# State-space scan turned so that features lie on the output partitions, with the z projections inside the scan and a shorter output stage

## The chip, the core and the metric

The kernel runs on one core of a Trainium2 chip. The metric is the device time of one launch in microseconds. Engines are called by the names of the profile: PE is TensorE's matmuls, PEld its weight loads, DVE is VectorE, ACT is ScalarE, POOL is GpSimd, SP is the queue that issues most transfers.

## The reference, cut to what matters

One encoder layer runs over two sequences of 256 and 512 tokens (768 in all, 6 tiles of 128), model width 1024. The part that the change touches is the state-space branch:

```python
xbc = silu(conv7(xbc) + conv_b)            # 2048 x-features, 512 B, 512 C
xs = xbc[:2048] -> (tokens, 4 groups, 8 heads, 64)
for each direction (forward, backward):
    dt = softplus(dt_raw + dt_bias);  a_cum = cumsum(-exp(a_log) * dt) in chunks of 128
    y_diag[l] = sum_s (C_l . B_s) * exp(a_cum[l] - a_cum[s]) * dt[s] * x[s]     # s on one side of l
    states    = B^T (exp(a_end - a_cum) * dt * x), carried from chunk to chunk
    y_off[l]  = exp(a_cum[l]) * C_l . h_in
y = (y_fwd + y_bwd + d_skip * xs) * silu(z)
s_out = rmsnorm(y, ssm_norm) @ w_out_ssm;  merged = sigmoid(gate_s) * s_out + sigmoid(gate_a) * a_out
```

Query, key and value projections, windowed attention, a second gated output, a mixing product with routing, and a mixture of 32 experts follow. They keep their instructions.

## The kernel before, in words

Every engine runs its own written-out program; semaphores order them. Every stage begins and ends with a barrier. The work comes as **pieces**: 128 output columns of a weight matrix, 128x1024 per partition. SP loads a piece, ACT rounds it to a high part (`round`, L446), an elementwise pass subtracts to get the low part (`lower`, L451, on POOL), and PE multiplies three ways (high by high, low by high, high by low: `products`, L164). A piece takes 48 matmuls, 24 with 256 moving columns and 24 with 512. There are two buffers: piece n+2 is rounded when PE has finished piece n.

`ssd_groups` runs over four groups of heads. A **prologue** projects and convolves the six tiles of group 0. Then each group has a **head** (transposes of x and B, the products of C with B, eight chunk states carried along the chain) and six **steps**, one for each chunk of 128 tokens. In step t:

- PE projects a tile of the next group, multiplies C by the entering states (L648), waits for `decay_ok`, and multiplies the decays by x (16 products, L654).
- POOL subtracts the cumulative sums (`differences`, L737), makes dt*x and skip*x (`inputs`, L746 and L748), and lowers a piece.
- DVE multiplies the decays by C.B (`decay`, L807), caps the differences (`cap`, L802), gathers the chunk's result (`output`, L814 to L820), and convolves the next group's tile (`convolve`, L790 and L794, seven passes over 774 elements).
- ACT moves the projection out of the banks (`leave`, L673), rounds a piece, applies silu (L681), and makes one exponential over 2048 elements (`decay`, L685).

Tokens lie on the partitions of y, which goes to memory. `ssm_branch` then has 40 pieces: 16 z tiles (each with six transposes of y, L1000), the first halves of w_out for eight output tiles between the two halves of z, and eight pairs of gate and second half. `GatedOutput` makes these pairs.

## Time and profile before

| | us |
|---|---|
| median of 3 runs (2384.92 to 2391.55) | 2385.72 |
| the profiled execution's own time | 2384.32 |
| its span | 2382.6 |
| PE busy | 1873.8 (79%) |
| DVE busy | 868.8 (36%) |
| POOL busy | 627.5 (26%) |
| ACT busy | 551.8 (23%) |
| mean granted clock of TensorE | 0.841 of 2.4 GHz |

The busy shares are averages over stages that have different limits; the scan and the output stage are read by themselves below. The profiled execution is 1.4 us under the median.

### The profile page before, as it was taken

What the parts mean: (1) busy time and instruction counts of PE and PEld (TensorE: products, weight loads), DVE (VectorE), ACT (ScalarE), POOL (GpSimd) and SP (SyncE); (2) the same over time, 40 slices, a digit from 0 to 9 for tenths busy, and PEclk for the clock granted to TensorE, in tenths of its full rate; (3) what the DMA queues carried; (4) which work ended last, traced back from release to release, by engine and by line L of the source; (5) the groups of instructions that cost most, each with busy time, mean ns of one, the idle gap of its engine ahead of it and who ended that gap; (6) DMA issues with size and microseconds to landing.
All of it is one profiled execution on the core that took longest, in us unless ns stands there. A gap on an engine that the chain in (4) does not pass through costs nothing. (4 is left out here: it accounts for less than half of the span.)

```text
span 2382.6 us, 24844 instructions
## 1 busy us (share of the span) xinstructions
PE 1873.8 (79%) x8894; PEld 1299.0 (55%) x8894; DVE 868.8 (36%) x1168; ACT 551.8 (23%) x935; POOL 627.5 (26%) x394
## 2 busy tenths in 40 slices
PE   4968688685798999989889888979657786777771
PEld 3746477473687787877667777754312222222220
DVE  2779789696721122217622222211310000000002
ACT  3223223132132132126544433101100000000000
POOL 4267374753843253221100002210020000000002
PEclk7978788887599999999955558999778889988886
DMA  3313322323232231211188002222389999999994
GB/s 108 101 37 83 84 62 57 93 67 84 79 100 66 67 95 53 62 47 42 44 182 172 1 1 71 62 100 71 124 343 404 385 404 398 407 395 413 391 401 164
DMA packets 228718, 376.18 MB, mean 158 GB/s; under 512 B 9072, under 2 KB 185328, under 8 KB 219824
## 3 DMA queue, kind: packets, MB, share of 16 engines
q1 hardware_dynamic: 221504, 351.90, 43.2%
q0 software_dynamic: 6720, 21.50, 2.4%
q10 hardware_dynamic: 432, 1.96, 0.2%
q8 instruction: 37, 0.61, 0.1%
q14 instruction: 25, 0.20, 0.0%
HBM read 324.81 MB, written 48.96 MB: 157 GB/s over the span
## 5 line engine op out<-in xcount | busy, mean ns | idle before, releaser
L1898 PE MATMUL bank<-e_w,e_xT 128*64 128x512 f32 x1088 | 288.2, 690 | 125.3 <-DMA e_w<-in_w_up 123.9
L164 PE MATMUL bank<-h_high,w_w_high 128*128 128x256 f32 x960 | 342.3, 357 | 35.4 <-issue 7.7
L164 PE MATMUL bank<-h_low,w_w_high 128*128 128x256 f32 x960 | 332.6, 346 | 0.0
L164 PE MATMUL bank<-h_high,w_w_low 128*128 128x256 f32 x960 | 331.3, 345 | 0.0
L451 POOL TENSOR_TENSOR w_w_low<-w_raw,w_w_high 128x1024 fp32r<-128x1024 f32 x76 | 192.1, 2529 | 483.3 <-ACT w_w_high L446 483.3
L1898 PEld LDWEIGHTS bank<-e_w,e_xT 128*64 128x64 f32 x1088 | 92.9, 158 | 299.3 <-issue 232.6
L164 PEld LDWEIGHTS bank<-h_high,w_w_high 128*128 128x128 f32 x960 | 192.5, 200 | 64.5 <-issue 38.8
L794 DVE SCALAR_TENSOR_TENSOR ssd_xc<-ssd_conv_in,ssd_conv_p,ssd_xc 128x774 f32<-128x774 f32 x144 | 205.6, 1428 | 10.8
L164 PEld LDWEIGHTS bank<-h_low,w_w_high 128*128 128x128 f32 x960 | 192.4, 200 | 18.8 <-issue 2.4
L164 PEld LDWEIGHTS bank<-h_high,w_w_low 128*128 128x128 f32 x960 | 191.6, 200 | 19.3
L1956 POOL DMA_DIRECT2D rows_out<-e_y x68 | 36.3, 534 | 554.3 <-ACT e_y L1951 552.3
L654 PE MATMUL bank<-ssd_x_dt,ssd_decays 128*128 128x64 f32 x768 | 125.3, 341 | 48.2 <-DVE ssd_decays L807 41.0
L654 PEld LDWEIGHTS bank<-ssd_x_dt,ssd_decays 128*128 128x128 f32 x768 | 123.2, 255 | 67.6 <-DVE ssd_decays L807 50.5
L737 POOL TENSOR_TENSOR ssd_decays<-ssd_decays,ssd_tables 128x1024 f32<-128x1024 f32 x48 | 114.8, 2413 | 120.3 <-DMA ssd_decays<-decay_sums 120.3
L451 POOL TENSOR_TENSOR att_out_w_low<-att_out_raw,att_out_w_high 128x1024 fp32r<-128x1024 f32 x16 | 39.0, 2442 | 364.7 <-ACT att_out_w_high L446 364.7
L1918 PE MATMUL bank<-e_wd,e_actT 128*64 128x512 f32 x544 | 123.5, 596 | 1.7 <-issue 1.7
L685 ACT ACTIVATE ssd_decays<-ssd_decays 128x2048 f32<-128x2048 f32 x24 | 45.9, 1911 | 315.4 <-DVE ssd_decays L802 315.4
L1946 ACT ACTIVATE e_silu<-bank 128x256 f32<-128x256 f32 x34 | 13.0, 383 | 410.4 <-PE bank L1898 410.4
L446 ACT ACTIVATE w_w_high<-w_raw 128x1024 fp32r<-128x1024 f32 x76 | 80.6, 1061 | 118.6 <-PEq L460 114.7
L1925 DVE COPY e_xT<-bank 128x512 f32<-128x512 f32 x34 | 21.9, 686 | 225.4 <-PE bank L1886 225.4
L1485 PEld LDWEIGHTS bank<-v,att_pT 128*128 128x128 f32 x448 | 103.0, 322 | 0.0
L1932 DVE TENSOR_TENSOR e_act<-e_silu,bank 128x256 f32<-128x256 f32 x34 | 14.2, 416 | 241.6 <-ACT e_silu L1946 241.6
(253 smaller groups left out, 3068.2 us busy)
## 6 DMA issues: line engine op xcount, KB each, us to landing
e_w<-in_w_gate SPq DMA_DIRECT2D x34, 2048.0 KB, 15.1
e_w<-in_w_up SPq DMA_DIRECT2D x34, 2048.0 KB, 19.6
e_wd<-in_w_down SPq DMA_DIRECT2D x34, 2048.0 KB, 10.8
w_raw<-in_w_in SPq DMA_DIRECT2D x60, 512.0 KB, 4.6
ssd_decays<-decay_sums SPq DMA_DIRECT2D x48, 512.0 KB, 5.8
rows_in<-zeros SPq DMA_DIRECT2D x4, 3584.0 KB, 43.6
e_x<-rows_in SPq DMA_DIRECT2D x17, 512.0 KB, 11.1
rows_out<-e_y POOLq DMA_DIRECT2D x68, 128.0 KB, 6.1
```

The source lines that it names most:

```text
L164: last = pe.matmul(out, lhs[k][a], rhs[k][b], start=(k == 0 and m == 0), stop=(k == n - 1 and m == 2))
L446: act.activation(self.pair[u].high[:, :, :], self.raw[u][:, :, :], ACT.Copy).then_inc(self.rounded, 1)
L451: pool.tensor_tensor(self.pair[u].low[:, :, :], self.raw[u][:, :, :], self.pair[u].high[:, :, :].bitcast(F32), ALU.subtract).then_inc(self ...
L654: last = pe.matmul(core.bank[2 + t % 2][:, e * SP_:(e + 1) * SP_], decays[t % NDEC][:, d, e, :], x_dt[t % 2][:, d, e * SP_:(e + 1) * SP_], ...
L685: act.activation(decays[t % NDEC][:, :, :, :], decays[t % NDEC][:, :, :, :], ACT.Exp).then_inc(exp_ok, 1)
L737: last = pool.tensor_tensor(decays[t % NDEC][:, d, :, :], decays[t % NDEC][:, d, :, :], heads(table(g, "cum", t, d), P), ALU.subtract)
L794: last = dve.scalar_tensor_tensor(xc[:, ct, :], x[:, k:k + CONV], conv_p[:, ct, k:k + 1], xc[:, ct, :], ALU.mult, ALU.add)
L1485: last = pe.matmul(core.bank[4 + 2 * (t % 2) + head // 8][:, at:at + HD], pT[m % 4][:, b * P:(b + 1) * P], core.v[:, lo + b, kv * HD:(kv + ...
L1898: last = pe.matmul(core.bank[2 + u][half * CAP:(half + 1) * CAP, :], xT[:, k, u * CAP:(u + 1) * CAP], w[u][:, :, k, half * HALF:(half + 1) ...
L1918: last = pe.matmul(core.bank[6 + u][half * CAP:(half + 1) * CAP, :], act_T[u][:, k % 2, k // 2, :], wd[u][:, k, half * 512:(half + 1) * 51 ...
L1925: last = dve.tensor_copy(xT[:, 4 * j:4 * j + 4, :], core.bank[j][:, :].rearrange("p (k r) -> p k r", k=4))
L1956: pool.dma_start(core.rows_out[bass.ds(n * CAP, CAP), half * 512:(half + 1) * 512], y[u][half * CAP:(half + 1) * CAP, :]).then_inc(y_out[u ...
```

## The change

The scan is turned. x stays with its features on the partitions, and so does y. The diagonal part takes x of a head (128x64) as the weights and the decays (128 columns) as the moving operand; the two heads of a pair write partitions 0 to 63 and 64 to 127 of one bank. The entering states are weights in four blocks of 128x128, and C is the moving operand.

dt is taken into the exponent: a table `start` holds log dt minus the cumulative sum, and one exponential per head and direction takes it as its per-partition bias (16 passes over 128 elements in place of one over 2048). The cap becomes a minimum with the cumulative sum itself, so that POOL's subtraction goes, and so do dt*x; the skip is folded into x by ACT (four passes per group). exp(a_cum) comes from memory, copied over 64 partitions (`reach`).

POOL has nothing left in the scan and the output stage: lowering the pieces, making `x_end` and summing the squares go to DVE. The 16 z pieces move from the stage behind into the scan, by the list `ssd_schedule`; y is multiplied by silu(z) there, and goes to memory transposed. The stage behind, `ssm_output`, loads y in 16 tiles without transposing it, and has 24 pieces, over three pairs of banks. The scan is written out in full instead of in a loop over two of its groups.

At the start of the kernel the constants and the row of parameters are loaded in part; the rest comes in the query stage and the mixing stage. `step_sizes` makes one more logarithm and writes exp(a_cum) to memory.

```diff
+def ssd_schedule():
+
+    prologue = [("c", 0, ct) for ct in range(GC)]
+    prepare = [[] if g == 0 else [("z", g - 1, 2), ("z", g - 1, 3)] for g in range(SG)]
+    steps = []
+    for g in range(SG - 1):
+        c = [("c", g + 1, ct) for ct in range(GC)]
+        z = [("z", g, hp) for hp in range(2)]
+        steps.append([c[0:2], c[2:3], [c[3], z[0]], c[4:5], c[5:6], z[1:2]])
+    steps.append([[("z", SG - 1, hp)] for hp in range(4)] + [[], []])
+    return prologue, prepare, steps
...
+                def project(n, s):
+
+                    if s == 0:
+                        w.ready(pe, n)
+                    if n >= 2:
+                        pe.wait_ge(left, 2 * (n - 2) + s + 1)
+                    last = products(pe, core.bank[2 * (n % 2) + s][:, 0:SEQS[s]], w.parts(n % 2),
+                                    h_parts(core, FIRST[s] * P, SEQS[s]))
+                    last.then_inc(proj_mm if s == 0 else w.used, 1)
+
+                def both(piece):
                     for s in range(2):
-                        pe.wait_ge(left, 2 * (GC * g + ct) + s + 1)
-                        last = products(pe, core.bank[s][:, 0:SEQS[s]], w.parts(ct % 2),
-                                        h_parts(core, FIRST[s] * P, SEQS[s]))
-                        last.then_inc(proj_mm, 1)
...
+                def chunk(g, t):
+                    if t == 0:
+                        pe.wait_ge(cb_ok, 2 * g + 2)
+                        pe.wait_ge(st_ok, NST * g + NST)
+                    else:
+                        pe.wait_ge(y_ok, NT * g + t)
+                    for d in ENTERED[t]:
+                        for q in range(HP):
+                            pe.matmul(core.bank[6 + d][:, q * P:(q + 1) * P],
+                                      state[:, ENTERS[t, d], q * P:(q + 1) * P], xc[g % 2][:, POS[t]:POS[t] + P],
+                                      start=True, stop=True)
+                    pe.wait_ge(decay_ok, NT * g + t + 1)
+                    for q in range(HP):
+                        for d in range(2):
+                            for e in range(2):
+                                h = 2 * q + e
+                                last = pe.matmul(core.bank[4 + t % 2][SP_ * e:SP_ * (e + 1), q * P:(q + 1) * P],
+                                                 xs[:, t, h * SP_:(h + 1) * SP_], decays[t % 2][:, d, h, :],
+                                                 start=(d == 0), stop=(d == 1))
+                    last.then_inc(y_mm, 1)
+
+                for piece in PROLOGUE:
+                    both(piece)
+                for g in range(SG):
+                    if g:
+                        both(PREPARE[g][0])
+                    transposes(g)
+                    states(g, range(0, 3))
+                    if g:
+                        project(NUMBER[PREPARE[g][1]], 0)
+                    states(g, range(3, 6))
+                    if g:
+                        project(NUMBER[PREPARE[g][1]], 1)
+                    states(g, range(6, NST))
                     for t in range(NT):
-                        if more:
-                            project(g + 1, t)
-                        if t >= 2:
-                            pe.wait_ge(y_ok, NT * g + NT + t - 1)
-                        for d in range(2):
-                            if (t, d) in ENTERS:
-                                pe.matmul(core.bank[off_banks(t)[d]][:, :], cT[:, POS[t]:POS[t] + P],
-                                          state[:, ENTERS[t, d], :], start=True, stop=True)
-                        pe.wait_ge(decay_ok, NT * g + t + 1)
-                        pe.wait_ge(xdt_ok, NT * g + t + 1)
-                        for e in range(HPG):
-                            for d in range(2):
-                                last = pe.matmul(core.bank[2 + t % 2][:, e * SP_:(e + 1) * SP_],
-                                                 decays[t % NDEC][:, d, e, :],
-                                                 x_dt[t % 2][:, d, e * SP_:(e + 1) * SP_],
-                                                 start=(d == 0), stop=(d == 1))
-                        last.then_inc(y_mm, 1)
-
-                pe.sem_inc(y_mm, NT)
-                for ct in range(GC):
-                    project(0, ct)
-                groups(pe, scan)
+                        for piece in STEPS[g][t]:
+                            both(piece)
+                        chunk(g, t)
...
                 def decay(g, t):
                     act.wait_ge(capped, NT * g + t + 1)
-                    act.activation(decays[t % NDEC][:, :, :, :], decays[t % NDEC][:, :, :, :], ACT.Exp).then_inc(exp_ok, 1)
...
+                    for d in range(2):
+                        for h in range(HPG):
+                            at = g * HPG + h
+                            e = decays[t % 2][:, d, h, :]
+                            last = act.activation(e, e, ACT.Exp, bias=core.tab["start"][:, t, d, at:at + 1])
+                    last.then_inc(exp_ok, 1)
...
                 def cap(g, t):
 
-                    dve.wait_ge(diff_ok, NT * g + t + 1)
-                    flat = decays[t % NDEC][:, :, :, :].rearrange("p d e l -> p (d e l)")
-                    dve.tensor_scalar(flat, flat, 0.0, None, ALU.min).then_inc(capped, 1)
+                    dve.wait_ge(sums_in[t % 2], 16 * (NT // 2 * g + t // 2 + 1))
+                    to = core.tab["cum"][:, t, :, g * HPG:(g + 1) * HPG].unsqueeze(3).to_broadcast([P, 2, HPG, P])
+                    dve.tensor_tensor(decays[t % 2][:, :, :, :], decays[t % 2][:, :, :, :], to, ALU.min)\
+                        .then_inc(capped, 1)
 
                 def decay(g, t):
                     dve.wait_ge(exp_ok, NT * g + t + 1)
-                    for d in range(2):
-                        last = dve.tensor_tensor(decays[t % NDEC][:, d, :, :], decays[t % NDEC][:, d, :, :],
-                                                 cb[:, d, t, :].unsqueeze(1).to_broadcast([P, HPG, P]), ALU.mult)
-                    last.then_inc(decay_ok, 1)
+                    dve.tensor_tensor(decays[t % 2][:, :, :, :], decays[t % 2][:, :, :, :],
+                                      cb[:, :, t, :].unsqueeze(2).to_broadcast([P, 2, HPG, P]), ALU.mult)\
+                        .then_inc(decay_ok, 1)
 
...
                 def output(g, t):
...
+                    i = NT * g + t
...
+                    out = xx[g % 2][:, :, POS[t]:POS[t] + P]
+                    tiles = "p (q l) -> p q l"
+                    dve.wait_ge(y_mm, i + 1)
...
+                        dve.tensor_tensor(part[:, :].rearrange(tiles, l=P), core.bank[6 + d][:, :].rearrange(tiles, l=P),
+                                          reach[t % 2][:, d, :, :], ALU.mult)
+                        if n == 0:
+                            dve.tensor_tensor(out, out, core.bank[4 + t % 2][:, :].rearrange(tiles, l=P), ALU.add)
+                        dve.drain()
+                        last = dve.tensor_tensor(out, out, part[:, :].rearrange(tiles, l=P), ALU.add)
+                        dve.drain()
                     last.then_inc(y_ok, 1)
...
+                def gate(g, hp):
+                    dve.wait_ge(left, 2 * NUMBER["z", g, hp] + 2)
+                    out = xx[g % 2][:, hp, :]
+                    dve.tensor_tensor(out, out, gate_tile(g, hp), ALU.mult).then_inc(gated, 1)
...
+                    for t in range(NT):
+                        decay(g, t)
+                        pieces = STEPS[g][t]
+                        if pieces:
+                            lower_ahead(pieces[0])
+                        if t:
+                            output(g, t - 1)
+                        elif g:
+                            gate(g - 1, 3)
+                        if t + 1 < NT:
+                            cap(g, t + 1)
+                        if len(pieces) > 1:
+                            lower_ahead(pieces[1])
+                        if g + 1 < SG:
+                            convolve(g + 1, t)
+                    dve.drain()
+                output(SG - 1, NT - 1)
+                for hp in range(HP):
+                    gate(SG - 1, hp)
...
+def output_order():
+
+    order = [("gate", 0), ("gate", 1)] + [("half", c) for c in range(D // P)] + [("gate", 2)]
+    for c in range(D // P):
+        order.append(("branch", c))
+        if c + 3 < D // P:
+            order.append(("gate", c + 3))
+    return order
```

VectorE in step 1 of a group. In the names, `ssd_decays` holds the decays of the chunk, `ssd_y` (before) and `ssd_x` (now) the output, and L790/L794 and L842/L845 are the convolution. Before:

```order
L807 TENSOR_TENSOR ssd_decays<-ssd_decays,ssd_cb 128x1024 [waits ssd_exp_ok]
L807 TENSOR_TENSOR ssd_decays<-ssd_decays,ssd_cb 128x1024
L802 TENSOR_SCALAR ssd_decays<-ssd_decays 128x2048 [waits ssd_diff_ok]
L814 TENSOR_TENSOR ssd_y<-ssd_y,bank 128x512 [waits ssd_y_mm]
L817 TENSOR_TENSOR ssd_part<-bank,ssd_tabs 128x512
L820 TENSOR_TENSOR ssd_y<-ssd_y,ssd_part 128x512
L790 TENSOR_SCALAR ssd_xc<-ssd_conv_in,ssd_conv_p 128x774 [waits ssd_left]
L794 SCALAR_TENSOR_TENSOR ssd_xc<-ssd_conv_in,ssd_conv_p,ssd_xc 128x774 x6
```

and now:

```order
L857 TENSOR_TENSOR ssd_decays<-ssd_decays,ssd_cb 128x2048 [waits ssd_exp_ok]
L466 TENSOR_TENSOR w_w_low<-w_raw,w_w_high 128x1024 [waits piece_rounded]
L873 TENSOR_TENSOR ssd_part<-bank,ssd_reach 128x512 [waits ssd_reach_in0,ssd_y_mm,ssd_dsc_ok]
L876 TENSOR_TENSOR ssd_x<-ssd_x,bank 128x4x128
L878 TENSOR_TENSOR ssd_x<-ssd_x,ssd_part 128x4x128
L852 TENSOR_TENSOR ssd_decays<-ssd_decays,ssd_cum 128x2048 [waits ssd_sums_in0]
L842 TENSOR_SCALAR ssd_x<-ssd_conv_in,feat 128x774 [waits ssd_y_out,ssd_left]
L845 SCALAR_TENSOR_TENSOR ssd_x<-ssd_conv_in,feat,ssd_x 128x774 x6
```

The subtraction that lowers a piece (L466) has come in ahead of the output of the chunk before, and it waits for `piece_rounded`. The cap (L852) waits for the transfer and not for POOL, and now stands behind the output. A pass over the 2048 decays is one instruction.

TensorE in step 1, from the end of the projection to the next one. The names are those of the operands, `ssd_state` the entering states. Before:

```order
L164 MATMUL bank<-h_low,w_w_high 128x512
L164 MATMUL bank<-h_high,w_w_low 128x512
L648 MATMUL bank<-ssd_state,ssd_cT 128x512
L650 REGISTER_ALU
L654 MATMUL bank<-ssd_x_dt,ssd_decays 128x64 [waits ssd_xdt_ok,ssd_decay_ok]
L654 MATMUL bank<-ssd_x_dt,ssd_decays 128x64 x15
L456 REGISTER_ALU
L596 ISA [waits piece_split]
L164 MATMUL bank<-h_high,w_w_high 128x256 [waits ssd_left]
```

and now:

```order
L165 MATMUL bank<-h_low,w_w_high 128x512
L165 MATMUL bank<-h_high,w_w_low 128x512
L708 MATMUL bank<-ssd_xc,ssd_state 128x128 [waits ssd_y_ok]
L708 MATMUL bank<-ssd_xc,ssd_state 128x128 x3
L716 MATMUL bank<-ssd_decays,ssd_xs 64x128 [waits ssd_decay_ok]
L716 MATMUL bank<-ssd_decays,ssd_xs 64x128 x15
L165 MATMUL bank<-h_high,w_w_high 128x256 [waits ssd_left,piece_split]
L165 MATMUL bank<-h_low,w_w_high 128x256
```

The products with the entering states now wait for `ssd_y_ok` of the chunk before (step 1 had no such wait, later steps waited for the chunk two before). The diagonal products write 64 partitions of 128 columns in place of 128 of 64.

## Rows read from the trace of the kernel before

**Rows 1.** Windows: stretch and length, busy us (count) per engine, clock, DMA share, GB/s.

```profile
66.00:140.00 74.00, 59.62 (x329) 50.90 (x330) 58.45 (x53) 23.27 (x35) 24.23 (x10) 0.90 0.36 93
...
274.00:419.00 145.00, 112.67 (x549) 90.79 (x547) 122.01 (x98) 40.31 (x47) 84.36 (x44) 0.83 0.27 74
...
564.00:657.00 93.00, 59.44 (x224) 41.97 (x224) 61.52 (x54) 13.36 (x8) 73.17 (x41) 0.61 0.34 93
657.00:1045.00 388.00, 359.46 (x2020) 307.16 (x2020) 91.56 (x100) 102.90 (x134) 137.86 (x57) 0.98 0.25 70
```

**Rows 2.** Groups of instructions: busy us, mean ns, idle before and releaser.

```profile
L794 DVE SCALAR_TENSOR_TENSOR ssd_xc<-ssd_conv_in,ssd_conv_p,ssd_xc 128x774 f32<-128x774 f32 x144 | 205.6, 1428 | 10.8
...
L451 POOL TENSOR_TENSOR w_w_low<-w_raw,w_w_high 128x1024 fp32r<-128x1024 f32 x76 | 192.1, 2529 | 483.3 <-ACT w_w_high L446 483.3
```

**Rows 3.** Timeline of VectorE, 533 to 548 us, GpSimd idle: start, duration.

```profile
533.23 1.22 DVE L802 TENSOR_SCALAR ssd_decays<-ssd_decays 128x2048 f32<-128x2048 f32 x1
...
534.37 0.68 DVE L814 TENSOR_TENSOR ssd_y<-ssd_y,bank 128x512 f32<-128x512 f32 x1
...
536.49 0.69 DVE L817 TENSOR_TENSOR ssd_part<-bank,ssd_tabs 128x512 f32<-128x512 f32 x1
...
538.04 0.68 DVE L790 TENSOR_SCALAR ssd_xc<-ssd_conv_in,ssd_conv_p 128x774 f32<-128x774 f32 x1
538.80 6.52 DVE L794 SCALAR_TENSOR_TENSOR ssd_xc<-ssd_conv_in,ssd_conv_p,ssd_xc 128x774 f32<-128x774 f32 x6
545.24 2.35 DVE L807 TENSOR_TENSOR ssd_decays<-ssd_decays,ssd_cb 128x1024 f32<-128x1024 f32 x2
```

**Rows 4.** Timelines of a head and of a step, 295 to 330 us: start, duration, idle before.

```profile
295.80 1.04 POOL L757 TENSOR_TENSOR ssd_x_end<-ssd_xs,ssd_tables 128x512 f32<-128x512 f32 x1 [1.34 <-PE bank L636]
296.89 1.13 PE L636 MATMUL bank<-ssd_x_end,ssd_b 128*128 128x512 f32 x2 [0.48 <-POOL ssd_x_end L757]
...
311.28 1.12 PE L648 MATMUL bank<-ssd_state,ssd_cT 128*128 128x512 f32 x2
311.30 0.85 ACT L673 ACTIVATE ssd_conv_in<-bank 128x256 f32<-128x256 f32 x2
...
312.04 1.06 ACT L446 ACTIVATE w_w_high<-w_raw 128x1024 fp32r<-128x1024 f32 x1
312.24 3.68 PE L654 MATMUL bank<-ssd_x_dt,ssd_decays 128*128 128x64 f32 x32
...
329.40 1.99 PE L654 MATMUL bank<-ssd_x_dt,ssd_decays 128*128 128x64 f32 x10 [3.85 <-DVE ssd_decays L807]
```

**Rows 5.** Timeline of TensorE in two projections at 2.4 GHz.

```profile
905.23 0.39 PE L164 MATMUL bank<-ssm_y_low,w_w_high 128*128 128x512 f32 x1
905.46 0.39 PE L164 MATMUL bank<-ssm_y_high,w_w_low 128*128 128x512 f32 x1
...
912.53 0.28 PE L164 MATMUL bank<-h_high,w_w_high 128*128 128x256 f32 x1
912.65 0.28 PE L164 MATMUL bank<-h_low,w_w_high 128*128 128x256 f32 x1
```

**Rows 6.** Windows around a wait of TensorE and at the scan's end.

```profile
325.50:329.40 3.90, 0.05 (x2) 0.00 (x1) 3.90 (x3) 0.00 (x0) 3.90 (x3) 1.00 0.00 0
329.90:340.10 10.20, 10.20 (x50) 10.20 (x50) 9.05 (x9) 7.03 (x7) 5.35 (x3) 0.50 0.33 101
...
592.70:640.50 47.80, 39.08 (x142) 30.97 (x142) 36.19 (x26) 9.94 (x6) 43.74 (x24) 0.50 0.29 83
```

**Rows 7.** Timeline of TensorE in the expert stage: 18 records of 64-column halves, two alternating.

```profile
1804.81 4.04 PE L1898 MATMUL bank<-e_w,e_xT 128*64 128x512 f32 x18
```

**Rows 8.** Groups of ScalarE passes without and with a per-partition operand.

```profile
L1047 ACT ACTIVATE ssm_y_high<-ssm_zs,feat 128x768 f32 x16 | 15.0, 937 | 8.8 <-DVE ssm_zs L1110 8.8
...
L1051 ACT ACTIVATE ssm_square<-ssm_zs 128x768 f32<-128x768 f32 x16 | 13.3, 828 | 0.0
...
L1520 ACT ACTIVATE att_sunk<-att_sunk 128x4 f32<-128x4 f32 x24 | 4.7, 198 | 9.2 <-DVE att_sunk L1564 9.2
```

**Rows 9.** Timelines: VectorE's first pass, and TensorE where two stages begin.

```profile
12.79 1.42 DVE L263 TENSOR_SCALAR norm_h<-x_all,norm_rstd 128x1024 f32<-128x1024 f32 x2 [12.79 <-DMA row<-in_rows]
...
657.38 0.58 PE L164 MATMUL bank<-h_high,w_w_high 128*128 128x256 f32 x1 [7.43 <-ACTq L1054]
...
1045.43 0.55 PE L164 MATMUL bank<-h_high,w_w_high 128*128 128x256 f32 x1 [4.91 <-ACTq L1343]
```

999 lines of the change are left out of this document (529 added, 470 removed).

## The prediction

> **What bounds the kernel now.** I read the windows by stage first [rows 1]. The scan, 66 to 657 us, is 591 us long; in one of its groups (274 to 419 us, 145 us) VectorE is busy for 122.0, TensorE for 112.7 at a mean clock of 0.83, GpSimd for 84.4. The stage behind it takes 388 us, and TensorE is busy for 359.5 of them at 0.98: that one is plain TensorE time. So two things are to be read: what a step of the scan waits for, and what a piece costs on TensorE.
>
> The groups say that a convolution pass takes 1.428 us on average and a lowering 2.529 on GpSimd [rows 2]. In a stretch of the last group where GpSimd stands still, six such passes take 6.52 us, 1.09 each [rows 3]. VectorE is thus slowed while GpSimd works: seven passes take some 10.8 us in the ordinary steps and 7.2 there. The step's timeline shows who waits: TensorE stood still for 3.85 us ahead of its diagonal products, released by VectorE's decays [rows 4]. A step takes 19 to 20 us, and VectorE's row of passes fills it.
>
> A projection costs 24 records at 0.23 us (512 columns) and 24 at 0.12 (256 columns), together 8.35 us at 2.4 GHz [rows 5]. The clock is the second matter. Before the 3.90 us in which TensorE did nothing the granted clock was 1.00; in the 10.2 us that followed it was 0.50 while TensorE was busy all the time [rows 6]. Such a stretch stands behind every gap of 3 us or more of the scan, and this one is among the shortest. At half clock 10.2 us do the work of 5.1, so a gap costs its own length and 5.1 us more.
>
> **VectorE and GpSimd.** POOL's work goes away, so I cost VectorE at the undisturbed durations [rows 3]: decay 2.28 (2.35 with its gap), convolution 7.2, output 0.7 a pass, three passes for one direction (2.15) and five for two (3.65). Two prices aren't in the trace. The subtraction of a piece (1024 elements, both operands in memory) is between half of the two-operand pass over 2048 (1.15) and GpSimd's 2.53; I take 1.25 from the near end. The cap is now a two-operand pass: not under the 1.22 of the one-operand pass, and not over the 2.35 of the decay's pass, which has its shape; I take 2.28. The Trainium skill ("VectorE: DVE Perf Modes", the tables of measured times) gives 2293 ns for a two-operand float pass of 2048 and 1227 for a one-operand one; the row of L802 agrees with the second, and by the first the cap would come out as here.
>
> Per one-piece step VectorE has 2.28 + 1.25 + 2.15 to 3.65 + 2.28 + 7.2, so 15.2 to 16.7; a group's sum, head included, is about 120 us. Per group that is no more than before, although the lowering has come over. VectorE alone would allow steps of 16 us.
>
> **TensorE's step.** It has no slack of the old kind, for the orders show a new chain. Its state products wait for `y_ok` of the chunk before; VectorE makes that output behind the lowering of the next piece; the lowering waits for ACT's rounding; and that waits until the projection is over. After the projection's last product follow: leaving the bank and rounding, 0.6 + 1.06 [rows 4], so 1.65; the lowering 1.25; the output 2.15 to 3.65. So TensorE stands still for 5.1 to 6.6 us in each one-piece step. Behind the wait it has the state products, a bank of 512 columns each (0.95 [rows 4]), and the diagonal. Those are 32 records of 128 columns. One alone should take 0.12, a quarter of the 0.5 that a record over 512 takes in L648, and 32 of the old ones took 3.68 [rows 4]; so 3.6 in a row. But they write halves of a bank's partitions in turn. In the expert stage 18 such records of 512 columns take 4.04, 0.45 a pair [rows 7], while a whole-width record over 512 costs 0.5 by [rows 4]: the two halves run beside one another. So I take 1.8; the bounds are 1.8 and 3.6.
>
> Steps at full clock: projection 8.35 (16.7 with two pieces), gap 5.1 to 6.6, state products 0.9 to 1.8, diagonal 1.8. With two pieces the wait is hidden partly. The six steps are 19.4, 16.3, 19.4, 17.2, 18.6 and 17.7, together 108.6. Four of the gaps are over 3 us and each costs 5.1: 20 more, so **129 us for six steps**.
>
> **Heads.** A head is VectorE's now. It makes eight `x_end` (1.04 each on GpSimd [rows 4]; I take the same), eight carries of 0.69 and four multiplies of 0.9, masks 1.95, cap 2.28, two lowerings, an output and three gates of 1.1, some 30 us, and waits for six transposed tiles and the z piece ahead of them, 6 more. Two z pieces of TensorE (16.7) fit under it, as does the product of a state, 1.0 [rows 4]. With the clock's loss of 5 to 8 a head takes 41; a **middle group 170** where it took 145 and did two z pieces less in its head and two less in its steps.
>
> **ScalarE.** Sixteen exponentials take the place of one of 1.9 us. A pass over 4 elements takes 0.198 [rows 8]; the 124 further elements add 0.10 at 0.83 us per 768 wide pass; a per-partition operand costs 0.937 against 0.828, so 0.11 more. That is 0.41 each and 6.6 a chunk; bounds 0.3 and 0.41, so 4.8 and 6.6. It runs while VectorE convolves for 7.2, and would be late only in the last group, where nothing is convolved: 4 us, counted there. [...]
>
> **The sum.** The prologue and the first head end at 156 (152 before: ACT has rounding, skip and 16 passes there). 156 + 129 + 170 + 170, and for the last group 160 (head 41, six steps of 11 to 18 us, 92 in all, 12 for the clock, 5 for its gates, 10 for the last transfer and the barrier): TensorE starts the output stage at 785 + 4 for a last gap's clock = 789, where it did at 657.4 [rows 9]: **132 us later**. The output stage has 24 pieces instead of 40: 24 x 8.35 = 200, + 5 at half clock in the beginning, + 1.5 where the first loads of y come late, + 1.3 before the second product, + 4.9 until the next stage's first product, which the trace shows now [rows 9]: 213, where it was 388. **175 less.** 789 + 213 = 1002 against 1045.4: 43 less.
>
> At the start VectorE's first pass waits until 12.79 for the row of parameters [rows 9], which is cut to a fraction: -3 at the most, I take -2. `step_sizes` has one more logarithm, one more exponential and two more transfers in a row at its end: +4. The late loads of constants lie beside work, +1. So -40 against the profiled execution's 2384.3: 2344, and 1.4 more for the median: **2345**.
>
> **The rivals.**
> *No clock lost* (0.17). TensorE has 81 us of products in a group's six steps and head against 170; if gaps of 5 us don't bring the clock down, 20 for steps and 5 to 8 for heads vanish in each of three groups: -80, **2265**. For it: the clock is 0.90 in the prologue, with shorter gaps. Against: [rows 6], and each other gap.
> *The halves run one after the other* (0.13). The diagonal then costs 1.8 more in each of 24 chunks, 43 and with half clock 50: **2393**. Against it stands [rows 7], where the operands are of the same kind. The Trainium skill ("TensorEngine Tiling (Array Packing)", the key properties) says that tiles work independently, but that a change of the mode first needs a drain; here each step changes from whole width to halves and back. By it some fractions of a us a step come on top.
> *Slower: the clock stays down* (0.15). At the scan's end TensorE was at 0.50 for all of 47.8 us while busy for 39.1 [rows 6]. With a gap of 5 to 7 us in every step the next one may come before the clock has risen. All of a group's products at half clock cost 80 more, 60 more than counted, so 215 over the scan: **2560**. It decides as soon as a fifth of that happens, which is when TensorE is at 1.2 GHz for some 80 us more than I count in four groups. Against it: the stretch after the single gap ended after 10.2 us, before the next gap.
> *VectorE bounds the steps* (0.05): if `output` from transposed banks, the lowering or the cap is 1 us dearer, steps grow by about that beyond a slack of 1 us, +25, **2370**.
>
> **Numbers.** The forecast has 0.50. A change under 0.3%, 7 us, counts as none. Faster: 0.50 + 0.17 + 0.03 of the rest; same 0.08 and slower 0.22, the halves' case and the clock's. The forecast's own range is 2310 to 2375 (diagonal, lowering and head at their bounds). The range to 8 in 10 takes in the case of no lost clock and the halves, not the clock that stays down: 2257 to 2400.
>
> **What would show it.** GpSimd idle in the scan; passes of the convolution at 1.03 to 1.09; 32 diagonal records in about 1.8 to 2; an idle time of 5 to 7 us ahead of L708, ended by `ssd_x`; granted clock in the groups 0.8 to 0.85; a group period of 170; 213 for the output stage with TensorE over 97% busy. Wrong would be: a clock near 0.5 through the steps, gaps under 3 us, or a stage behind that waits for its loads of y.

## The result and the profile after

| | us |
|---|---|
| kernel before, median of 4 runs (2383.52 to 2391.55) | 2385.32 |
| changed kernel, median of 4 runs (2269.09 to 2283.05) | 2271.97 |
| ratio | 0.9529, 95% interval 0.9492 to 0.9566 |
| span of the profiled execution | 2267.4 |
| mean granted clock | 0.852 |

The change made the kernel 113 us faster. The forecast had the direction, but only 40 us. The windows of the changed kernel (columns as in [rows 1]) say where the rest lies: prologue and first chunk, a middle group from one last diagonal product to the next, the last group with the stage's end, and the output stage.

```profile
64.40:165.90 101.50, 86.91 (x483) 71.79 (x483) 71.92 (x90) 36.55 (x65) 0.00 (x0) 0.94 0.26 73
262.90:416.40 153.50, 126.81 (x797) 107.70 (x795) 112.39 (x115) 75.67 (x156) 0.00 (x0) 0.90 0.32 100
570.00:708.90 138.90, 96.28 (x603) 81.08 (x603) 75.05 (x78) 59.92 (x136) 0.00 (x0) 0.84 0.29 91
708.90:925.10 216.20, 206.54 (x1156) 180.71 (x1157) 85.88 (x93) 73.21 (x96) 0.00 (x0) 0.98 0.30 88
```

A middle group takes 153.5 us with its four z pieces (145 before with none [rows 1], 170 forecast), and TensorE is busy for 126.8 of them at a clock of 0.90, where it had 0.83. GpSimd has nothing to do. The output stage takes 216.2 us (388 before, 213 forecast). The two rows of TensorE with which the output stage and the next one begin stand against [rows 9] (657.38 and 1045.43):

```profile
708.87 0.55 PE L165 MATMUL bank<-h_high,w_w_high 128*128 128x256 f32 x1 [9.31 <-PEq L579]
```

```profile
925.12 0.55 PE L165 MATMUL bank<-h_high,w_w_high 128*128 128x256 f32 x1 [5.80 <-ACTq L1466]
```

So the scan ends 51.5 us later than before, where 132 had been forecast, and the output stage ends 120 us earlier (1045.4 before, 925.1 now). The later stages take 5 us more.

The groups (busy, mean ns, idle before and releaser) have the prices that the prediction had to bound:

```profile
L783 ACT ACTIVATE ssd_decays<-ssd_decays,ssd_start 128x128 f32<-128x128 f32 x384 | 115.1, 390 | 48.6 <-DVE ssd_decays L852 48.5
...
L845 DVE SCALAR_TENSOR_TENSOR ssd_x<-ssd_conv_in,feat,ssd_x 128x774 f32<-128x774 f32 x96 | 98.5, 1026 | 7.5 <-issue 0.4
...
L466 DVE TENSOR_TENSOR w_w_low<-w_raw,w_w_high 128x1024 fp32r<-128x1024 f32 x64 | 78.4, 1225 | 228.8 <-ACT w_w_high L461 228.8
...
L716 PE MATMUL bank<-ssd_decays,ssd_xs 128*64 128x128 f32 x768 | 59.7, 321 | 0.0
L708 PE MATMUL bank<-ssd_xc,ssd_state 128*128 128x128 f32 x256 | 56.0, 398 | 96.6 <-DVE ssd_x L878 96.6
L852 DVE TENSOR_TENSOR ssd_decays<-ssd_decays,ssd_cum 128x2048 f32<-128x2048 f32 x24 | 54.9, 2290 | 1.5
...
L901 DVE TENSOR_TENSOR ssd_x_end<-ssd_xs,ssd_to_end 128x512 f32<-128x512 f32 x32 | 21.9, 685 | 2.4 <-ACT ssd_xs L789 2.4
```

A convolution pass takes 1.025 us everywhere (1.428 on average before [rows 2]). Lowering on VectorE takes 1.225, the cap 2.290, an exponential with its bias 0.300 on average (16 times 0.300 is 4.80). `x_end` takes 0.685 on VectorE and took 1.04 on GpSimd [rows 4]. The Trainium skill ("VectorE: DVE Perf Modes", the perf-mode tier table) has 2293 ns for the cap's kind of pass, and the trace agrees. The Trainium skill ("ScalarE: Activation LUTs", "What ACT_TABLE_LOAD costs") gives a pass with a per-partition bias 280 ns and 0.833 ns a column, of which 93 ns overlap where passes follow one another. An estimate from that page is 0.29 us each and 4.7 us for the sixteen, and the trace agrees with 4.80.

The timeline of a one-piece step shows the chain that the prediction described (start, duration, idle before and releaser):

```profile
365.14 0.60 ACT L763 ACTIVATE ssd_conv_in<-bank 128x512 f32<-128x512 f32 x1 [0.55 <-PE bank L165]
365.64 1.05 ACT L461 ACTIVATE w_w_high<-w_raw 128x1024 fp32r<-128x1024 f32 x1
...
366.72 1.23 DVE L466 TENSOR_TENSOR w_w_low<-w_raw,w_w_high 128x1024 fp32r<-128x1024 f32 x1 [0.34 <-ACT w_w_high L461]
367.86 0.69 DVE L873 TENSOR_TENSOR ssd_part<-bank,ssd_reach 128x512 f32<-128x512 f32 x1
...
368.46 0.68 DVE L876 TENSOR_TENSOR ssd_x<-ssd_x,bank 128x512 f32<-128x512 f32 x1
...
369.21 0.69 DVE L878 TENSOR_TENSOR ssd_x<-ssd_x,ssd_part 128x512 f32<-128x512 f32 x1
...
369.96 3.78 PE L708 MATMUL bank<-ssd_xc,ssd_state 128*128 128x128 f32 x16 [4.86 <-DVE ssd_x L878]
...
373.67 2.30 PE L716 MATMUL bank<-ssd_decays,ssd_xs 128*64 128x128 f32 x32
```

The bank is left at 365.7, the weights are rounded at 366.7, lowered at 367.9, the output is written at 369.9, and only then TensorE begins the state products, after 4.86 us. This is the chain of the forecast with its lengths. Four more windows of the same step show its clock (the column ahead of the last two):

```profile
365.20:367.50 2.30, 0.00 (x0) 0.00 (x0) 1.96 (x2) 2.28 (x3) 0.00 (x0) 1.00 0.00 0
367.70:369.90 2.20, 0.00 (x0) 0.00 (x0) 2.13 (x4) 2.17 (x3) 0.00 (x0) 0.50 0.20 47
370.00:374.30 4.30, 4.30 (x22) 4.08 (x24) 4.15 (x4) 2.12 (x8) 0.00 (x0) 0.50 0.81 207
374.50:378.00 3.50, 3.50 (x45) 3.33 (x42) 3.28 (x4) 2.62 (x9) 0.00 (x0) 1.00 0.26 80
```

TensorE stops at 365.1. The clock falls to 1.2 GHz at 367.6, 2.4 us before the gap ends, and is back at 374.4. Of these 6.8 us some 4.4 fall on work, and so the fall costs 2.2 us. The prediction had taken 5.1 from [rows 6], where the fall came right behind a gap of 3.9 us. Two things differ: the stretch at 1.2 GHz is 6.8 us long and not 10.2, and a part of it is idle time. Behind sixteen of the seventeen gaps of the steps it is 6.8 us long, behind one 3.4; on average 4.4 us of it are work.

The kernel before had stretches of all these lengths, of which the prediction read the one of 10.2. These windows show the stretches that came with gaps of 3.0 and 4.0 us, and the greater part of the one that came with a gap of 6.4 us:

```profile
302.60:306.00 3.40, 3.40 (x16) 3.21 (x16) 2.15 (x1) 0.00 (x0) 3.40 (x2) 0.50 0.00 0
155.80:162.60 6.80, 5.18 (x24) 5.18 (x25) 6.63 (x5) 0.00 (x0) 6.80 (x3) 0.50 0.00 0
515.30:524.40 9.10, 9.10 (x43) 9.10 (x44) 8.10 (x7) 7.03 (x7) 4.29 (x3) 0.50 0.08 30
```

They cost 1.7, 2.6 and 4.6 us (half of the work in the whole stretch). The gap of the last was as long as the gaps of 6.39 us now, which cost 1.7 to 2.0. So the length of a gap does not give the price, and why the stretches are shorter now stays open.

### The profile page after: what moved, and what is told of

The parts are those of the page before. It is cut to its first block and busy times, and to the rows that moved or that the text cites. A ratio compares the mean times of both kernels' runs of the same rounds, so it can differ in the third digit from the quotient of the medians.

```text
span 2267.4 us, 24076 instructions
## 1 busy us (share of the span) xinstructions
PE 1780.7 (79%) x8990; PEld 1245.8 (55%) x8990; DVE 829.1 (37%) x1222; ACT 659.9 (29%) x1336; POOL 155.6 (7%) x161
## 5 line engine op out<-in xcount | busy, mean ns | idle before, releaser
L2025 PE MATMUL bank<-e_w,e_xT 128*64 128x512 f32 x1088 | 288.0, 690 | 132.9 <-DMA e_w<-in_w_up 131.5
L165 PEld LDWEIGHTS bank<-h_high,w_w_high 128*128 128x128 f32 x960 | 184.7, 192 | 49.0 <-issue 31.1
L466 DVE TENSOR_TENSOR w_w_low<-w_raw,w_w_high 128x1024 fp32r<-128x1024 f32 x64 | 78.4, 1225 | 228.8 <-ACT w_w_high L461 228.8
L708 PE MATMUL bank<-ssd_xc,ssd_state 128*128 128x128 f32 x256 | 56.0, 398 | 96.6 <-DVE ssd_x L878 96.6
L783 ACT ACTIVATE ssd_decays<-ssd_decays,ssd_start 128x128 f32<-128x128 f32 x384 | 115.1, 390 | 48.6 <-DVE ssd_decays L852 48.5
L708 PEld LDWEIGHTS bank<-ssd_xc,ssd_state 128*128 128x128 f32 x256 | 51.2, 299 | 104.1 <-DVE ssd_x L878 103.5
L1679 DVE CUSTOM_DVE_ANT_0 att_score<-bank,late 128x256 f32<-128x256 f32 (+1 forms) x96 | 41.4, 467 | 163.9 <-PE bank L1595 163.9
L845 DVE SCALAR_TENSOR_TENSOR ssd_x<-ssd_conv_in,feat,ssd_x 128x774 f32<-128x774 f32 x96 | 98.5, 1026 | 7.5 <-issue 0.4
L1609 PE MATMUL bank<-v,att_pT 128*128 128x64 f32 x448 | 101.1, 386 | 0.0
L1790 PE MATMUL bank<-mix_wo,mergedT 128*128 128x512 f32 x192 | 86.6, 611 | 13.1 <-DMA mix_wo<-in_w_o 13.1
L466 POOL TENSOR_TENSOR w_w_low<-w_raw,w_w_high 128x1024 fp32r<-128x1024 f32 x12 | 28.8, 2400 | 984.5 <-ACT w_w_high L461 984.5
```

Source lines behind the costliest of these rows:

```text
L165: last = pe.matmul(out, lhs[k][a], rhs[k][b], start=(k == 0 and m == 0), stop=(k == n - 1 and m == 2))
L466: pool.tensor_tensor(self.pair[u].low[:, :, :], self.raw[u][:, :, :], self.pair[u].high[:, :, :].bitcast(F32), ALU.subtract).then_inc(self ...
L708: pe.matmul(core.bank[6 + d][:, q * P:(q + 1) * P], state[:, ENTERS[t, d], q * P:(q + 1) * P], xc[g % 2][:, POS[t]:POS[t] + P], start=True ...
L783: last = act.activation(e, e, ACT.Exp, bias=core.tab["start"][:, t, d, at:at + 1])
L845: last = dve.scalar_tensor_tensor(out, x[:, k:k + CONV], p[k], out, ALU.mult, ALU.add)
L1609: last = pe.matmul(core.bank[4 + 2 * (t % 2) + head // 8][:, at:at + HD], pT[m % 4][:, b * P:(b + 1) * P], core.v[:, lo + b, kv * HD:(kv + ...
```

## The experiments

All times of starts and stretches are of the profiled execution; the output stage starts at 708.9 in the changed kernel. Differences in microseconds are taken against its median of 2271.97. The kernel before, run again beside each set of experiments, had medians of 2377.6 to 2382.2 where it had 2385.3 beside the changed kernel, so a difference of medians of less than some 8 us is not read.

**Output ahead of the decays.** VectorE's order within a step:

```diff
+                        if t:
+                            output(g, t - 1)
                         decay(g, t)
                         pieces = STEPS[g][t]
                         if pieces:
                             lower_ahead(pieces[0])
-                        if t:
-                            output(g, t - 1)
-                        elif g:
+                        if g and t == 0:
                             gate(g - 1, 3)
```

> VectorE makes the output of the chunk before ahead of the decays and the lowering, not behind them. Theory chain (a one-piece step of 19.4 to 20.7 us is set by projection, leave and round 1.65, lowering 1.23, output 2.06 to 3.6, state products, diagonal): the state products start right behind the projection, the wait moves in front of the diagonal products and is 2.4 to 4 us, a one-piece step falls by about 3 us, 13 such steps give 40: about 2232 us. Rival sum (VectorE's own passes fill the step, only their order changes): 2265 to 2272.

Measured: 2192.47 us (2190.18 to 2194.87), 0.9209 of before (0.9156 to 0.9262). That is 80 us under the changed kernel, twice what the chain theory gave. The output stage starts at 633.9, 75 us earlier. TensorE in the step that took 19.07 us in the changed kernel:

```profile
311.35 1.16 PE L708 MATMUL bank<-ssd_xc,ssd_state 128*128 128x128 f32 x8 [0.74 <-DVE ssd_x L878]
313.73 1.97 PE L716 MATMUL bank<-ssd_decays,ssd_xs 128*64 128x128 f32 x32 [1.23 <-DVE ssd_decays L857]
```

and the stretch from the first chunk of this group to that of the next:

```profile
302.10:438.30 136.20, 121.58 (x795) 102.80 (x795) 111.46 (x116) 75.29 (x157) 0.00 (x0) 0.96 0.37 113
```

The waits are 0.74 and 1.23 us in place of 4.86, and this step takes 13.6 us. I had let it shrink by its own wait alone, to 16 us. But of the 5.5 us only 2.9 are waiting; the rest is the clock, whose fall had cost 2.8 in this step. The stretch is 136.2 us long, of which TensorE is idle for 14.6 and busy for 121.6; from the same place to the same place it was 153.5, with 26.7 idle and 126.8 busy. So a group gives back 12 us of idle time and 5 of the clock.

The expectation had 13 waits; the trace of the changed kernel has 17 ahead of state products, and over all of them 57 us of idle time go, about 3.3 us a wait. The chain theory thus had the size of one wait right. It missed four waits and the clock. The order that it names is a circle: TensorE waited for VectorE's output, which stood behind a lowering that waited for TensorE's projection.

**The gap filled with products.** Added ahead of the wait for the output:

```diff
                     else:
+                        if len(STEPS[g][t]) < 2:
+                            for _ in range(18):
+                                pe.matmul(core.bank[4 + t % 2][:, 0:P], core.ident, core.ones, start=True, stop=True)
                         pe.wait_ge(y_ok, NT * g + t)
```

> Adds work: 18 products of 128 columns (about 4 us) on TensorE into the bank that the diagonal writes next, ahead of the wait for the output, in steps with fewer than two pieces. They fill the gaps of 4.86 to 7.5 us. Theory clock (a gap costs its length and 2 to 3 us more because TensorE runs at 1.2 GHz behind it, some 35 us in the steps): the granted clock stays at 1.0 in the steps and the kernel comes to about 2237 us. Rival (the chain hides the slower products, or the rest of the gap is enough to bring the clock down): 2268 to 2275.

Measured: 2234.3 us (2221.97 to 2249.79), 0.9368 (0.9306 to 0.943). More work, less time. TensorE in one step (the first row is the added work), and a middle group:

```profile
357.45 4.18 PE L707 MATMUL bank<-const 128*128 128x128 f32 x36
362.47 2.05 PE L711 MATMUL bank<-ssd_xc,ssd_state 128*128 128x128 f32 x16 [0.83 <-DVE ssd_x L881]
364.45 1.97 PE L719 MATMUL bank<-ssd_decays,ssd_xs 128*64 128x128 f32 x32
```

```profile
313.00:459.60 146.60, 136.06 (x939) 117.91 (x939) 112.06 (x115) 75.58 (x157) 0.00 (x0) 0.98 0.34 105
```

The gap that is left is 0.83 us, the clock is 0.98 in the group, the state products take 2.05 for two directions, which at 1.2 GHz took 3.78, and the output stage starts at 686.9, 22 us earlier. The clock's part in the scan is 27 us, of which the added work takes back 5. The medians differ by 38, but the profiled execution (span 2248.1) is the longest of the four; where the others gained more, no trace shows.

**Half of the filling.** The same with `range(9)`.

> Adds 9 products (2 us) in TensorE's gaps where the run with the full fill had 18, so that 2.9 to 4.4 us of each gap stay. Theory place (a gap of 3 to 4 us still brings the clock down, and then, as in the kernel before, the whole stretch at 1.2 GHz falls on work behind the gap, while in a gap of 5 to 7 us it begins inside the gap): no gain over the unfilled kernel or a loss, 2270 to 2295 us. Rival (the loss goes with the length of the idle time): half of the full fill's gain, 2253 us.

Measured: 2268.49 us (2244.86 to 2268.82), 0.9522 (0.9465 to 0.9578). The output stage starts at 709.2, where the unfilled kernel has 708.9: two of five microseconds of idle time are gone and nothing is gained. TensorE in one step, then the group and the stretch behind the gap:

```profile
365.38 2.17 PE L707 MATMUL bank<-const 128*128 128x128 f32 x18
370.39 2.65 PE L711 MATMUL bank<-ssd_xc,ssd_state 128*128 128x128 f32 x16 [2.85 <-DVE ssd_x L881]
372.97 2.98 PE L719 MATMUL bank<-ssd_decays,ssd_xs 128*64 128x128 f32 x32
```

```profile
318.10:471.40 153.30, 134.72 (x867) 116.07 (x867) 112.10 (x115) 75.63 (x157) 0.00 (x0) 0.92 0.32 100
...
372.00:376.00 4.00, 4.00 (x38) 3.60 (x38) 3.78 (x5) 3.24 (x12) 0.00 (x0) 0.61 0.52 130
```

State and diagonal products together take 5.6 us behind the gap of 2.85 and took 6.1 behind the gap of 4.86; at 2.4 GHz they take 4.0. The stretch at 1.2 GHz is now shorter: behind this gap it is 3.4 us long (371.7 to 375.1), where it was 6.8. But it begins when TensorE works again, so all of it falls on work. Over the six steps of all groups and the heads between them the clock costs 40.6 us here and 41.9 in the unfilled kernel. That is what the theory of the place said of the sum, though it had the stretch as long as before.

**The halves one after the other.**

```diff
-                    for q in range(HP):
+                    for e, q in [(e, q) for e in range(2) for q in range(HP)]:
                         for d in range(2):
-                            for e in range(2):
                                 h = 2 * q + e
```

> The diagonal products of a chunk in another order: first all that write partitions 0 to 63, then all that write 64 to 127. Theory pairs (32 records take 1.97 us because the two halves run beside one another when they alternate): now 3.6 us a chunk, 24 x 1.7 = 40 more, 2312 us. Rival (a record with 64 rows of weights is short by itself, whatever its neighbour): no change, 2272.

Measured: 2302.52 us (2300.91 to 2306.19), 0.9677 (0.9621 to 0.9732), 31 us over the changed kernel. One chunk at full clock:

```profile
164.69 3.33 PE L715 MATMUL bank<-ssd_decays,ssd_xs 128*64 128x128 f32 x32
```

Alternating, the same 32 records take 1.97. So the pair rule read from [rows 7] is right, and the rival would have cost 33 us, not 43. No cost of the change between whole width and halves shows: in the changed kernel the first chunk's state products start at 162.95, its diagonal at 163.94 and the next projection at 165.83, one behind the other.

**Lowering on GpSimd again.**

```diff
                 def lower_ahead(piece):
-                    n = NUMBER[piece] + 2
-                    if n < len(ORDER) + 2:
-                        w.lower(dve, n, n % 2)
+                    pass
...
+            @block.gpsimd
+            def _(pool):
+                for n in range(2, len(ORDER) + 2):
+                    w.lower(pool, n, n % 2)
```

> The lowering of the pieces in the scan goes back to GpSimd; all else as in the changed kernel (a spill of y also waits for the spill before it). Theory chain: VectorE's output is no longer behind the lowering, a one-piece step's gap is 1.2 us shorter, and GpSimd's 2.5 us are hidden behind state and diagonal products; passes of VectorE beside it are slower, inside the slack: 2255 us. Rival contention (what the change gained was VectorE's freedom from GpSimd): convolution passes at 1.2 to 1.4 us in place of 1.03, steps 1 to 2 us longer, 2295 us.

Here each spill of y (its transfer to memory) also waits for the one before.

Measured: 2216.91 us (2210.96 to 2225.52), 0.9319 (0.9259 to 0.9378): 55 us under the changed kernel.

```profile
L466 POOL TENSOR_TENSOR w_w_low<-w_raw,w_w_high 128x1024 fp32r<-128x1024 f32 x52 | 140.5, 2702 | 819.2 <-ACT w_w_high L461 819.2
...
L850 DVE SCALAR_TENSOR_TENSOR ssd_x<-ssd_conv_in,feat,ssd_x 128x774 f32<-128x774 f32 x96 | 118.2, 1231 | 7.2
```

Both theories were half right. The convolution passes are slower (1.231), as the rival said, and the prologue's first chunk ends 5 us later. But the lowering no longer stands between TensorE's projection and VectorE's output, which opens the same circle as the first experiment: three of the four one-piece steps of a group fall to 11 to 14 us, while step 4 stays at 20 to 22, with a wait of 6.1. Between the first chunk and the last 45 us of idle time and 22 of the clock are gone. So moving the lowering to VectorE, which I had put down as a relief, cost 55 us as the change placed it. With the spills issued one after the other, the last takes 5 us longer here.

**Both of these.** Output first and the lowering on GpSimd.

> Output first, and the lowering of the scan's pieces on GpSimd too. Theory sum (with the output first VectorE's own passes are next to be the bound; 9.8 us of lowering a group go, but its other passes are 0.1 to 0.2 us slower each beside GpSimd): 2185 to 2200 us, no gain over output first alone. Rival chain (the lowering's wait for the rounding still sits on the path): 2165 us.

Measured: 2206.66 us (2205.32 to 2207.1), 0.9294 (0.9272 to 0.9317). That is 14 us more than output first alone, and above the expected 2185 to 2200. By the traces none of it lies in the groups, which are 5 us shorter from the first chunk to the last (453.3 against 458.0). The first chunk ends 5 us later, the scan's end takes 4 us more by the spills issued one after the other, and what lies behind the scan, where the two kernels are the same, is 7.5 us longer. So this run doesn't show that the lowering is better placed on VectorE.

**No z pieces.** The list without them, and no projection, rounding or silu for them:

```diff
-    prepare = [[] if g == 0 else [("z", g - 1, 2), ("z", g - 1, 3)] for g in range(SG)]
+    prepare = [[] for g in range(SG)]
...
-        steps.append([c[0:2], c[2:3], [c[3], z[0]], c[4:5], c[5:6], z[1:2]])
-    steps.append([[("z", SG - 1, hp)] for hp in range(4)] + [[], []])
+        steps.append([c[0:2], c[2:3], c[3:4], c[4:5], c[5:6], []])
+    steps.append([[] for t in range(6)])
```

> Leaves the 16 z pieces out altogether (no projection, no rounding and lowering of them, no silu; the output is multiplied by itself in the place of silu(z), so VectorE keeps that pass). 16 pieces are 134 us of TensorE at full clock. Theory hidden (a middle group is bound by VectorE in the head and by the chain in the steps, so that most of a z piece lies beside them): about 10 us less in each of three groups and 22 in the last, 52 in all, 2220 us; then the pieces cost 52 here where they cost 134 and more in the stage behind. Rival plain (the scan's TensorE time counts in full): 2138 us.

Measured: 2319.03 us, which can't be compared as a whole, since other values go to other experts and what lies behind the scan is 120 us longer. The scan can: the output stage starts at 644.8, 64 us earlier, although its end takes 5 us more by spills issued one after the other, as above. A middle group:

```profile
260.60:397.10 136.50, 97.29 (x602) 80.27 (x602) 107.03 (x111) 65.88 (x142) 0.00 (x0) 0.86 0.31 97
```

Without four pieces a group takes 136.5 in place of 153.5: 4.2 us a piece, half of what its products take. So 16 pieces cost 64 to 72 us in the scan (52 expected); in the stage behind their products alone are 134. Between the first chunk and the last, this run has 131 us less of TensorE's work, 48 more of idle time and 12 more lost to the clock: the other half of the pieces had stood in idle time.

**One part of the change in the kernel before.** The pieces of the scan lowered by VectorE:

```diff
+                        if more and t + 2 < GC:
+                            lower(g + 1, t + 2)
+                        if ahead and t + 2 >= GC:
+                            lower(g + 2, t + 2 - GC)
                         if more:
                             convolve(g + 1, t)
```

> The kernel before with one part of the change alone: the pieces of the scan are lowered by VectorE ahead of its convolution, not by GpSimd. Theory small (VectorE gets 1.25 us a step more and its passes are beside GpSimd for 2.5 us less): within 10 us of before, 2375 to 2395. Rival contention (the lowering on GpSimd is what slowed VectorE): 2350 us or less.

Measured: 2375.1 us (2360.26 to 2385.09), 0.9982 (0.995 to 1.0013): no change that can be told.

```profile
L786 DVE SCALAR_TENSOR_TENSOR ssd_xc<-ssd_conv_in,ssd_conv_p,ssd_xc 128x774 f32<-128x774 f32 x144 | 164.6, 1143 | 11.2 <-issue 0.6
```

The passes fall from 1.428 to 1.143 and VectorE has 41 us less in them, 30 us more in lowerings. The scan ends 8 us earlier, of which 3.7 are the prologue and 2.6 the groups. So the gain of the change doesn't come from this part by itself; which of GpSimd's other passes held the steps is not shown.

**One exponential.** The 16 passes replaced by one without bias.

> The changed kernel with one exponential over 2048 elements for the 16 with a bias (the table of log dt less the sum is left out, so the values are others and the routing of the experts may be too: it is read at the start of the output stage, 708.9 us in the changed kernel). Theory hidden (the 16 passes, 4.8 us together, lie beside the convolution; only the last three chunks wait for them): 6 to 9 us earlier, 700 to 703 us. Rival (they are on the path of each step): 3 us a chunk, 640 us.

Measured: the output stage starts at 706.3, 2.6 us earlier; the time of the whole is 2375.69, with other values and another routing.

```profile
L780 ACT ACTIVATE ssd_decays<-ssd_decays 128x2048 f32<-128x2048 f32 x24 | 45.9, 1913 | 49.7 <-DVE ssd_decays L849 49.6
```

One pass takes 1.913 and the sixteen 4.80, so 2.9 us a chunk are saved, 69 in all, and 2.6 arrive. The last group alone is 6.4 us shorter, as expected; the first chunk ends 0.9 later, the first group is 2.1 longer, with 2.4 more lost to the clock, and the end takes 0.6 more. In the two middle groups nothing changes (153.6 us each): there the passes are hidden.

**A later second lowering.** Output first, and

```diff
-                        if len(pieces) > 1:
-                            lower_ahead(pieces[1])
                         if g + 1 < SG:
                             convolve(g + 1, t)
+                        if len(pieces) > 1:
+                            lower_ahead(pieces[1])
```

> Output first, and in steps of two pieces the second lowering behind the convolution. Theory sum (VectorE stands still for 2.3 us in each two-piece step until the second piece is rounded, and is late for the two or three steps behind): the waits of 0.7 to 3.5 us ahead of the state products shrink, 6 to 8 us a group, about 2170 us. Rival (the second lowering comes too late for the piece that needs it): 2192 us or more.

Measured: 2192.04 us (2184.02 to 2195.7), 0.9202 (0.9184 to 0.9219). The output stage starts at 625.5, 8.4 us earlier than with output first alone, but the medians don't tell them apart. The waits of steps 1 and 3 are gone, and are found again in step 4:

```profile
356.77 3.78 PE L708 MATMUL bank<-ssd_xc,ssd_state 128*128 128x128 f32 x16 [5.21 <-DVE ssd_x L878]
360.49 2.65 PE L716 MATMUL bank<-ssd_decays,ssd_xs 128*64 128x128 f32 x32
```

VectorE is busy for 112 us of a group of 133, and is now late in step 4, and by 1.5 us in step 5.

**And filled.** 8 added products in steps 1, 4 and 5 (in the last group in 4 and 5).

> The same with 8 added products of 128 columns (1.8 us) ahead of the wait for the output in steps 1, 4 and 5, and in the last group in steps 4 and 5. [...] Rival place (gaps of 3 to 4 us stay, and bring the clock down as before): no gain, within 5 us.

Measured: 2191.22 us (2184.13 to 2195.78), 0.9183 (0.9157 to 0.921): no gain. Step 4 falls from 20.0 to 16.45 us, but step 1, which had no gap, pays 1.8 for its filling, and the step or head behind is longer by up to 2.3 us. The output stage starts 3.7 us later (629.2), although the clock costs 10 us less between the first chunk and the last.

## Why the prediction was wrong

**What bounds the kernel** was read rightly: the chain from projection to `y_ok` is there row by row, the gaps of 4.86 and 6.39 us are the forecast's 5.1 and 6.6, and the stage behind is TensorE's own time (216.2 against 213). The direction, the prices on VectorE (1.225, 2.290, 1.025), the diagonal in 1.97 (forecast 1.8) and the cover of the exponentials hold.

**The step that failed is "a gap costs its own length and 5.1 us more".** It costs its length and 2.2. The start of the output stage was put at 789 and came at 708.9, 80 us earlier. By the sum's own terms:

| | forecast | measured |
|---|---|---|
| prologue and first head end at | 156 | 146 |
| six steps of group 0 | 129 | 117 |
| a middle group, twice | 170 | 153.5 |
| last group with its end | 160 | 139 |
| last gap's clock, apart | 4 | 0 |

(The first row is the end of the first chunk, 165.9, less a two-piece step of 19.7.) Of the 12 us of the six steps all is the clock: 108.6 were forecast at full clock, and the four gaps cost 7.2 together and not 20. A middle group was 16.5 off. Its clock is 0.90 over 153.5 us, so it has 30.7 us at 1.2 GHz: four stretches of 6.8 and one of 3.4 in the head. Some 21 of them are work, so 10.5 are lost; the forecast had lost 25 to 28. That is nearly all of the 16.5, and what is left at full clock, 143, is what the forecast had (145). Over the scan the clock is thus some 50 of the 80 us. Filling shows the same from the other side: 22 us of the scan come back with 18 products a gap, and none with 9.

The 5.1 came from one stretch of 10.2 us that was all work, called "among the shortest". The kernel before had stretches of 3.4 and 6.8 us behind gaps of 3 us and more. The rival "no clock lost" named 2265, close to the result, but it isn't what happened: the clock falls behind every gap and costs less than half of what was forecast. Its number is close by luck: it takes 80 us from the clock, where some 50 came from there and the rest from the prologue and the last group. Its "81 us of products" in a group was also too low: ten pieces alone are 83.5, and the trace has 116 at full clock (126.8 busy less 10.5).

**Prologue.** I had taken 4 us more than before for ScalarE and none less for VectorE. In the prologue too the convolution was slowed by GpSimd (passes of 1.33 on average, 1.03 now), and with the lowering back on GpSimd the passes over x take 1.36 and the first chunk ends 5 us later, 1 of them by a later start of the scan. So 4 of the 10 us are shown; 1.6 more come from the earlier start of the scan, and the rest isn't split. That VectorE was slowed was in [rows 2] and was left out of the sum.

**Last group.** It is 21 us shorter than forecast: the head takes 35.4 where I had 41 (its clock costs 1.6, not 5 to 8), the end 9.3 with the gates where I had 15, and the six steps 94 where I had 104. Some 12 of the 94 are lost to the clock, as forecast; the exponentials, for which these steps wait, are 4.8 and not 6.6 a chunk, and the rest of the steps was counted too high by some 5. The 4 us of the last gap's clock did not come: the stretch at 1.2 GHz from 702.1 on has 0.1 us of work before the output stage starts.

**The lowering on VectorE** was counted at 1.25 us of VectorE and 1.25 of the chain. What it does is to tie VectorE to TensorE's projection, which the two orders show: 55 us by going back to GpSimd, 80 by going behind the output. The time from the end of the first chunk to that of the last, in three parts (work at full clock; the clock, which is half of the busy time at 1.2 GHz; idle time of TensorE), in us:

| | length | work | clock | idle |
|---|---|---|---|---|
| changed kernel | 533.7 | 382.6 | 41.9 | 109.1 |
| output first | 458.0 | 384.4 | 21.1 | 52.5 |
| lowering on GpSimd | 468.1 | 383.9 | 20.0 | 64.2 |
| both | 453.3 | 383.5 | 17.7 | 52.2 |
| gaps filled | 511.3 | 453.2 | 14.8 | 43.2 |
| half filled | 533.1 | 417.3 | 40.6 | 75.3 |

The prediction had this chain in front of it and priced the wait rightly. The experiments gained more than expected since there are 17 such waits and most bring a fall of the clock with them.

At the start VectorE's first pass comes 2.6 us earlier (10.22 against 12.79; 2 forecast), but the scan begins 1.6 us earlier (64.38 against 66.01) where the sum had it later: the step sizes and what lies around them take 1 us more, not 4. The runs that share this part begin the scan between 63.5 and 66.0, so this is read to a microsecond or so. The later stages take 5 us more in this execution, in the experts' waits for weights (131.5 us against 123.9); their cause stays open, as what lies behind the scan differs by 8 us among the runs that share it (1556.8 to 1564.9).

The best version has the output ahead of the decays: 2192 us, 0.921 of before. A later second lowering has the same median.

## What to carry to other kernels

Before you move a pass to an engine that seems free, ask what the pass waits for. If it waits for the engine that its new neighbours serve, it closes a circle, and every step costs the sum of both. Price a fall of the clock by the work that stands under it, and read several of the trace's stretches and not one: here they cost from 1.7 to over 5 us. Whether filling idle time pays has to be tried: 9 products a gap gained nothing, and 18 gained 22 us. Products that write the two halves of the partitions belong next to each other.

## What was not expected of the hardware

- Gaps of 2.85 us and of 4.86 lose nearly the same (40.6 and 41.9 us over the groups), and the stage behind started at the same time within 0.4 us.
- In the changed kernel the clock also fell behind a gap of 2.0 us in each of three heads, for 3.4 us, which cost 1.6.
- Added products (18 of 128 columns in each step with fewer than two pieces) made the scan 22 us shorter.
- 32 records of 64 rows of output take 1.97 us when the halves alternate and 3.33 when they don't, so a record takes 0.06 or 0.10.
- An exponential over 128 elements with a per-partition bias takes 0.30 us in a row of sixteen; 0.41 had been worked out from rows of single passes.
